# A diffusion trunk step on one core: prologue in three token spans, expert choice in two sorted halves between the output tiles, second norm applied to turned tiles

## The chip, the cores and the metric

The kernel runs on one core of one Trainium2 chip. The metric is device time in microseconds (us) of one execution; the time of a version is the median of several runs. TensorE (PE) does matrix products, VectorE (DVE) and ScalarE (ACT) element-wise work, GpSimd (POOL) here the indirect transfers and some adds, SyncE (SP) issues the other DMAs. The engines wait for each other through semaphores written out by hand.

## The reference

One layer over 128 context tokens and 1024 latent tokens of width 1024. What matters here is the start and the second half:

```python
mod = silu(cond) @ ada_w + ada_b
shift1, scale1, gate1, shift2, scale2, gate2 = split(mod, 6)
h = rmsnorm(x, norm1_g) * (1 + scale1) + shift1
proj = h @ w_in
...                                   # pooling branch, DeltaNet branch, merge -> mixed
x = x + gate1 * (mixed @ w_out)
h = rmsnorm(x, norm2_g) * (1 + scale2) + shift2
aff = softmax(h @ router_w)           # 16 experts
gates, idx = top_k(aff.T, cap)        # each expert picks cap = N/8 tokens of its set
ys = (silu(h[idx] @ w_gate) * (h[idx] @ w_up)) @ w_down * gates
x = x + gate2 * scatter_add(ys, idx)
```

Context and latent tokens have their own modulation (two condition vectors) and are separate routing sets: each of 16 experts picks 128 of 1024 latent tokens and 16 of 128 context tokens. A final RMSNorm follows. All is float32 but the inner solver of the DeltaNet.

## The kernel before

Tokens lie in nine tiles of 128 (tile 0 is context). The program is one long list per engine, and the order in each list is the order of execution.

**Prologue** (`prologue_pe`, `prologue_act`, `prologue_dve`, `sync1`). SP loads constants, then eight slabs of 1 MB of `ada_w` (set 0: shift1 and scale1), the nine tiles of x, the first head's weights, and sixteen more slabs (sets 1 and 2: gate1 and shift2, then scale2 and gate2), in a ring of four slots, so that slab n is issued when slab n-4 has been used. PE multiplies set 0; ACT computes the norms of all nine tiles (`act1`); PE turns the tiles so that channels lie on the partitions (`transpose_x`, three token spans of 128, 512 and 512, five banks); ACT and DVE apply scale and shift while they drain the banks (`modulate_act`, `modulate_dve`). Only when all are drained does PE start the first head's projections: units "q0" to "g1" of the tuple `FIRST` (letter: matrix, digit: span), with beta and alpha, decay sums and rows between them, and sets 1 and 2 at the end. `dve4_first` waits until sets 1 and 2 are written to `mod_dram`; ACT's drains of g0 and g1 wait for it.

**Heads, pooling, merge**: eight heads, and the mixed tensor. The change leaves their code alone.

**Step 7** (`pe7`, `act7`, `dve7`, `sync7`), for tile t = 0 to 8: PE projects tile t+1 (two halves of 512 columns); DVE multiplies by a broadcast row gate1 and adds x; ACT gets 1/rms; DVE multiplies by 1/rms and a row `amp2` and adds a row `shift2`; PE turns the result h2 (8 transposes); ACT drains it; PE multiplies it, as the stationary operand, by the router (16 columns). x goes to `x2_dram`, h2 to `h2_dram`.

**Step 8** (`dve8`, `act8`, `pe8`): softmax of all nine tiles at once, nine transposes, and then on DVE the choice over 16 partitions: 16 rounds over the 1024 latent tokens (maximum of 8, their indices, replace by -1), 2 rounds over the 128 context tokens.

**Step 9**, for each expert e: PE does 8 gate/up units, turns in the tokens of expert e+1 (`turn_in`), does 8 down units. ACT (`body9_act`) drains the turned tokens (`evac_in`) between its last Silu and the first drain of a down unit. The down units alternate between two banks: down unit 2 waits until ACT has drained down unit 0.

## Time and profile before

| | us |
|---|---|
| median of 3 runs | 2845.84 (2845.37 to 2846.87) |
| profiled execution, its own time | 2844.15 |
| its span in the trace | 2842.4 |
| PE busy in the span | 2577.6 (91%) |
| DVE busy | 1119.7 (39%) |
| ACT busy | 834.4 (29%) |

The span runs from the first to the last instruction of the trace. The busy shares are means over stages that have different limits; times below are counted from the start of the span. A matrix product in float32 shows as two records, so that a unit of eight products has "x16".

### The profile page before, as it was taken

The numbers are of one execution on the slowest core, as the hardware profiler recorded it, in microseconds if no ns is written. First come the engines' busy times: TensorE is split into PE (matmuls) and PEld (weight loads), VectorE is DVE, ScalarE is ACT, GpSimd is POOL, SyncE is SP. The second block draws the span as 40 slices with busy tenths as digits, with TensorE's granted clock in tenths as the row PEclk, the third lists the DMA queues.
The fourth block names the chain that finished last, engine by engine and source line by source line (L and its number), as shares of the span: only waits on it lengthen the run. The fifth ranks groups of instructions, "written<-read, shape, count | busy, mean of one in ns | idle before, by whom it ended". The sixth has DMA issues, their size and how long they took to land.

```text
span 2842.4 us, 42397 instructions
## 1 busy us (share of the span) xinstructions
PE 2577.6 (91%) x16072; PEld 1875.0 (66%) x16072; DVE 1119.7 (39%) x1996; ACT 834.4 (29%) x2081; POOL 303.2 (11%) x212
## 2 busy tenths in 40 slices
PE   5899999999989999899989999991799999999994
PEld 2355556565665656566555555440799999999994
DVE  2255565655656556565652353228110100101012
ACT  3133443444334353353442111110111112121112
POOL 0030030301203012030200000000010010101000
PEclk8999999999999999999999999995899999999997
DMA  8330200102002020110124233214478788787874
GB/s 294 149 94 19 73 17 18 58 19 73 17 24 64 6 73 17 55 36 3 59 85 153 96 114 104 96 74 185 174 247 296 263 279 303 248 299 247 293 268 150
DMA packets 197302, 365.30 MB, mean 129 GB/s; under 512 B 9006, under 2 KB 70387, under 8 KB 194083
## 3 DMA queue, kind: packets, MB, share of 16 engines
q1 hardware_dynamic: 190755, 344.41, 34.7%
q0 software_dynamic: 6400, 18.88, 2.7%
q8 instruction: 99, 1.62, 0.2%
q14 instruction: 48, 0.39, 0.0%
HBM read 322.59 MB, written 40.67 MB: 128 GB/s over the span
## 4 chain that ended last, share of the span: by engine, by line
PE 83%; DVE 6%; DMA 4%; issue 3%; ACT 2%; POOL 1%; SPq 1%; DVEq 0%; POOLq 0%; ACTq 0%
PE bank L563 25%; PE bank L1729 18%; PE bank L1743 9%; PE bank L733 6%; PE bank L1489 5%; PE bank L1277 4%; PE bank L1295 2%; PE bank L724 2%; DMA arena<-in_w_in 2%; PE bank L785 1%; PE bank L780 1%; PE bank L708 1%; PE bank L789 1%; PE bank L788 1%; DMA arena<-in_ada_w 1%
## 5 line engine op out<-in xcount | busy, mean ns | idle before, releaser
L563 PE MATMUL bank<-arena 128*128 128x512 f32 (+1 forms) x2496 | 874.1, 494 | 42.8 <-DVE arena L983 19.4
L563 PEld LDWEIGHTS bank<-arena 128*128 128x128 f32 x2496 | 394.1, 192 | 336.2 <-issue 298.7
L1729 PE MATMUL bank<-arena 128*128 128x144 f32 x4096 | 512.7, 286 | 1.5 <-ACT arena L1759 1.5
L1729 PEld LDWEIGHTS bank<-arena 128*128 128x128 f32 x4096 | 509.4, 190 | 1.7 <-ACT arena L1759 1.7
L1805 DVE TENSOR_TENSOR arena<-arena,bank 128x144 f32<-128x144 f32 x128 | 38.9, 304 | 702.7 <-ACT arena L1765 702.7
L873 ACT ACTIVATE arena<-bank 128x384 f16<-128x384 f16 (+1 forms) x504 | 205.9, 526 | 246.8 <-PE bank L724 246.6
L1743 PE MATMUL bank<-arena 128*128 128x144 f32 x2048 | 257.2, 286 | 0.7 <-DVE arena L1805 0.7
L1743 PEld LDWEIGHTS bank<-arena 128*128 128x128 f32 x2048 | 253.8, 189 | 1.9 <-DVE arena L1805 0.9
L733 PE MATMUL bank<-arena 128*128 128x128 f16 x2448 | 192.7, 220 | 6.5 <-ACT arena L873 0.2
L733 PEld LDWEIGHTS bank<-arena 128*128 128x128 f16 x2448 | 146.2, 98 | 67.9 <-ACT arena L873 36.8
L977 DVE CAST_PREDICATED arena<-arena,bank 128x384 f16<-128x384 uint32 x288 | 138.2, 553 | 99.5 <-PE bank L733 99.5
L1765 ACT ACTIVATE arena<-bank 128x144 f32<-128x144 f32 x128 | 37.2, 290 | 464.2 <-PE bank L1729 464.2
L594 ACT ACTIVATE arena<-bank 128x128 f32<-128x128 f32 (+1 forms) x156 | 77.1, 500 | 225.5 <-PE bank L563 185.4
L918 DVE SCALAR_TENSOR_TENSOR arena<-arena 128x1156 f32<-128x1156 f32 x96 | 136.3, 1420 | 5.9 <-issue 1.3
L1489 PE MATMUL bank<-arena 128*128 128x512 f32 x288 | 130.7, 614 | 1.7 <-DVE arena L1431 1.7
L969 DVE CAST arena<-bank 128x384 f16<-128x384 f32 x168 | 84.7, 552 | 118.4 <-PE bank L733 116.6
L1277 PE MATMUL bank<-arena 128*128 128x384 f32 x384 | 126.4, 491 | 0.7 <-DVE arena L1017 0.7
L1062 POOL TENSOR_TENSOR arena<-arena 128x1152 f32<-128x1152 f32 x8 | 29.5, 3689 | 826.2 <-ACT arena L895 826.2
L891 ACT ACTIVATE arena<-bank,arena 128x128 f32<-128x128 f32 x144 | 53.3, 370 | 190.9 <-PE bank L780 190.9
L1277 PEld LDWEIGHTS bank<-arena 128*128 128x128 f32 x384 | 73.4, 192 | 53.7 <-issue 3.2
L1489 PEld LDWEIGHTS bank<-arena 128*128 128x128 f32 x288 | 55.6, 195 | 70.9 <-issue 70.9
L1771 ACT ACTIVATE arena<-bank,arena 128x128 f32<-128x128 f32 x128 | 47.0, 367 | 177.3 <-PE bank L1743 177.3
(243 smaller groups left out, 2657.4 us busy)
## 6 DMA issues: line engine op xcount, KB each, us to landing
arena<-in_exp_w_gate SPq DMA_DIRECT2D x32, 2048.0 KB, 10.5
arena<-in_exp_w_up SPq DMA_DIRECT2D x32, 2048.0 KB, 15.6
arena<-in_exp_w_down SPq DMA_DIRECT2D x32, 2048.0 KB, 10.8
arena<-in_w_in SPq DMA_DIRECT2D x52, 512.0 KB, 6.8
arena<-in_ada_w SPq DMA_DIRECT2D x24, 1024.0 KB, 8.1
side_dram<-arena SPq DMA_DIRECT2D x20, 576.0 KB, 3.2
arena<-side_dram SPq DMA_DIRECT2D x20, 576.0 KB, 3.9
arena<-g_dram SPq DMA_DIRECT2D x16, 576.0 KB, 5.2
```

What stands on the lines that cost most here:

```text
L563: ins = nc.tensor.matmul(unit_bank(order, name)[:, 0:n], w[:, k, :], hT3[:, k, at:at + n], start=(k == 0), stop=(k == KD - 1))
L594: nc.scalar.activation(dst, bank[:, 0:n], ACT.Copy).then_inc(sem("pj_drained"), 1)
L724: last = nc.tensor.transpose(TRI[d][g].bitcast(F16)[:, i * P:(i + 1) * P], src[d][:, 3 * g + i, :], ident_h)
L733: last = nc.tensor.matmul(TRI[d][g][:, i * P:(i + 1) * P], lhs if lhs.shape[1] == P else lhs[:, 3 * g + i, :], rhs if rhs.shape[1] == P el ...
L873: nc.scalar.activation(flat(dst[d], g), src[:, 0:384], ACT.Copy).then_inc(sem(f"drained{d}_act"), 1)
L918: ins = nc.vector.scalar_tensor_tensor(qkvg[j][:, 0:CW], raw[j][:, tap:tap + CW], w, qkvg[j][:, 0:CW], ALU.mult, ALU.add)
L969: nc.vector.tensor_copy(flat(Zs[1], g), TRI[1][g][:, 0:384]).then_inc(sem("drained1_dve"), 1)
L977: nc.vector.copy_predicated(Ys[d][:, 3 * g:3 * g + 3, :], masks[:, 1 - d, lv + 1, :].unsqueeze(1).to_broadcast([P, 3, P]), TRI[d][g][:, 0: ...
L1277: last = nc.tensor.matmul(banks[n % RING][:, 0:CH], w_dn[half][:, k, col:col + P], bT3[:, k, c * CH:(c + 1) * CH], start=(k == 0), stop=(k ...
L1489: last = nc.tensor.matmul(banks[2 * (t % 2) + half][:, 0:512], mixT3[:, k, t * P:(t + 1) * P], w_outs[:, k, half * 512:(half + 1) * 512], ...
L1729: last = nc.tensor.matmul(banks[3 + f % 2][:, m * CAP:(m + 1) * CAP], w_unit[2 * half + m][:, k, col:col + P], xsT[:, k, :], start=(k == 0 ...
L1743: last = nc.tensor.matmul(banks[5 + dt % 2][:, 0:CAP], w_unit[4 + half][:, k, col:col + P], hid[:, k, :], start=(k == 0), stop=(k == KD - 1))
```

## The change

In the prologue each token span is normed, turned, drained and projected by itself, x tiles and head weights are loaded in that order, the slabs of sets 1 and 2 are multiplied in pieces between the projections, and only gate1 goes through `mod_dram`: shift2 and amp2 = (1 + scale2) * norm2_g are kept with channels on the partitions. In step 7 tiles run in the order 1 to 8, 0 (`TILE`); ACT writes x/rms, that is turned, and amp2 and shift2 are applied by ACT as scale and bias of eight ACTIVATEs per tile; the router is stationary in four groups of 32 columns, and `sel4` adds the four groups. The choice runs in three groups (tiles 1 to 4, 5 to 8, context), its rounds are written between the residuals of later tiles, and the two sorted lists of 128 are merged by one comparison of the first with the second read backwards. Since `xn_dram` holds x/rms alone, `evac_in` applies amp2 and shift2 to every expert's tokens too.

```diff
-        HB = 5
+        HB = 4
+        SPAN_USES = (range(0, KD), range(KD, 2 * KD), range(2 * KD, 3 * KD))
...
-        FIRST = ("q0", "q1", "q2", "v0", "v1", "v2", "k0", "k1", "k2", "g0", "g1")
+        FIRST = ("q0", "q1", "v0", "v1", "k0", "k1", "q2", "v2", "k2", "g0", "g1")
...
-            dve.wait_ge(sem("mod_saved"), 16 * NCG * (N_SETS - 1))
+            dve.wait_ge(sem("mod_saved"), 16 * (NCG // 2))
...
+        def turn_x(i):
+            pe.wait_ge(sem("xn_ready2"), i + 1)
...
+        def route(i):
+            pe.wait_ge(sem("h2T_ready"), i + 1)
             for k in range(KD):
-                last = nc.tensor.matmul(banks[6][:, t * E:(t + 1) * E], h2T[t % XR][:, k, :], router[:, k, :], start=(k == 0), stop=(k == KD - 1))
+                j = k % NCG
+                last = nc.tensor.matmul(banks[7][CG * j:CG * (j + 1), 0:P], router[:, k, :], h2T[i % XR][:, k, :], start=(k < NCG), stop=(k >= KD - NCG))
...
+        def logits(i):
+            pe.wait_ge(sem("routed_ready"), i + 1)
+            nc.tensor.matmul(LOGITS[:, i * E:(i + 1) * E], routed[i % 2], sel4[:, 0:E], start=True, stop=True).then_inc(sem("logits_filled"), 1)
...
+            nc.scalar.activation(xn_t[s], x_t[s], ACT.Copy, scale=rstd[i % 2]).then_inc(sem("xn_ready2"), 1)
+            if i == NL2:
+                routes_exp(act, 0)
+            act.wait_ge(sem("h2T_filled"), i + 1)
+            for k in range(KD):
+                last = nc.scalar.activation(h2T[s][:, k, :], banks[4 + k // 4][:, (k % 4) * P:(k % 4 + 1) * P], ACT.Identity,
+                                            scale=amp2T[:, c, k:k + 1], bias=modT3[:, c, 3 * KD + k:3 * KD + k + 1])
...
-            nc.vector.scalar_tensor_tensor(h2_t[s], x_t[s], rstd[t % 2], row["amp2"][c], ALU.mult, ALU.mult).then_inc(sem("h2_scaled"), 1)
-            nc.vector.tensor_tensor(h2_t[s], h2_t[s], row["shift2"][c], ALU.add).then_inc(sem("h2_ready"), 1)
...
+        for i in range(NL2 + 1):
+            residual(i)
+        shift_logits(0)
+        affinities(0)
+        take_affinities(0)
+        rounds(0, 0, 4)
+        residual(NL2 + 1)
+        rounds(0, 4, 10)
+        residual(NL2 + 2)
+        rounds(0, 10, ROUNDS)
+        residual(NL2 + 3)
+        step(nc.vector.tensor_copy(idxf3[0][0:E, :], idxu3[0][0:E, :]))
+        shift_logits(1)
+        affinities(1)
+        take_affinities(1)
+        rounds(1, 0, 2)
+        residual(2 * NL2)
+        rounds(1, 2, 8)
+        shift_logits(2)
+        affinities(2)
+        rounds(1, 8, ROUNDS)
+        take_affinities(2)
+        rounds(2, 0, CAP_C // 8)
...
     def evac_in(act, e):
         act.wait_ge(sem("xsT_filled"), e + 1)
-        for b in range(2):
-            nc.scalar.activation(xsT[:, 4 * b:4 * b + 4, 0:CAP_L], banks[b][:, 0:512].rearrange("p (k c) -> p k c", k=4), ACT.Copy)
-        for j in range(NJ):
-            last = nc.scalar.activation(xsT_c[:, :, j, :], banks[2][:, j * QROWS:(j + 1) * QROWS].rearrange("p (q c) -> p q c", q=NQ), ACT.Copy)
+        for k in range(KD):
+            nc.scalar.activation(xsT[:, k, 0:CAP_L], banks[k // 4][:, (k % 4) * P:(k % 4 + 1) * P], ACT.Identity,
+                                 scale=amp2T[:, 1, k:k + 1], bias=modT3[:, 1, 3 * KD + k:3 * KD + k + 1])
+        for k in range(KD):
+            q, j = k // NJ, k % NJ
+            last = nc.scalar.activation(xsT[:, k, CAP_L:CAP], banks[2][:, j * QROWS + q * CAP_C:j * QROWS + (q + 1) * CAP_C], ACT.Identity,
+                                        scale=amp2T[:, 0, k:k + 1], bias=modT3[:, 0, 3 * KD + k:3 * KD + k + 1])
         last.then_inc(sem("xsT_ready"), 1)
```

How the order moves, at three places. First PE in the prologue, from the end of set 0 on, before (L264 turns x, L563 is a projection, L330 beta and alpha):

```order
L264 MATMUL bank<-arena 128x128 x72
L563 MATMUL bank<-arena 128x128 x8
L563 MATMUL bank<-arena 128x512 x16
L330 MATMUL bank<-arena 32x128 x8
L330 MATMUL bank<-arena 32x512 x16
```

The same place in the change (L270 turns x, L584 is a projection, L244 a piece of a set, L336 beta and alpha):

```order
L270 MATMUL bank<-arena 128x128 x8
L584 MATMUL bank<-arena 128x128 x8
L270 MATMUL bank<-arena 128x128 x32
L584 MATMUL bank<-arena 128x512 x8
L584 MATMUL bank<-arena 128x128 x8
L584 MATMUL bank<-arena 128x512 x8
L244 MATMUL bank<-arena 32x512 x12
L584 MATMUL bank<-arena 128x128 x8
L584 MATMUL bank<-arena 128x512 x8
L270 MATMUL bank<-arena 128x128 x32
L336 MATMUL bank<-arena 32x128 x8
L336 MATMUL bank<-arena 32x512 x16
```

Five units of projection and three slabs now stand ahead of the last span's transposes. Second, PE in step 7, one tile before (L1489 output projection, L1501 transposes, L1505 router):

```order
L1489 MATMUL bank<-arena 128x512 x16
L1501 MATMUL bank<-arena 128x128 x8
L1505 MATMUL bank<-arena 128x16 x8
L1489 MATMUL bank<-arena 128x512 x16
L1501 MATMUL bank<-arena 128x128 x8
```

One tile in the change (L1566 half a projection, L1575 transposes, L1583 router in groups, L1589 their sum):

```order
L1566 MATMUL bank<-arena 128x512 x8
L1589 MATMUL bank<-arena 128x16
L1575 MATMUL bank<-arena 128x128 x8
L1566 MATMUL bank<-arena 128x512 x8
L1583 MATMUL bank<-arena 32x128 x8
```

Half a projection now lies between the transposes and the router that needs them drained. Third, ACT in step 9 between the last Silu of an expert and its first down units, before (L1757 and L1759 are `evac_in`, L1771 and L1772 the drain of a down unit):

```order
L1765 ACTIVATE arena<-bank 128x144
L1755 REGISTER_ALU
L1757 ACTIVATE arena<-bank 128x4x128 x2
L1759 ACTIVATE arena<-bank 128x4x16 x2
L1771 ACTIVATE arena<-bank,arena 128x128
L1772 ACTIVATE arena<-bank,arena 128x16
```

and in the change (L1915 and L1919 are `evac_in`, L1932 and L1933 the drain of a down unit):

```order
L1926 ACTIVATE arena<-bank 128x144
L1913 REGISTER_ALU
L1915 ACTIVATE arena<-bank,arena 128x128 x8
L1919 ACTIVATE arena<-bank,arena 128x16 x8
L1932 ACTIVATE arena<-bank,arena 128x128
L1933 ACTIVATE arena<-bank,arena 128x16
```

Sixteen instructions with scale and bias from memory stand where four plain copies stood.

## Rows read from the trace of the kernel before

**Rows 1.** Busy time by stretch (us): PE, PEld, DVE, ACT, POOL, PEclk, DMA share

```profile
1755.00:1927.00 172.00, 157.82 (x504) 82.46 (x504) 47.98 (x49) 24.61 (x54) 0.00 (x0) 0.94 0.21 77
2057.00:2107.00 50.00, 50.00 (x407) 49.76 (x406) 4.66 (x16) 9.18 (x29) 5.11 (x5) 1.00 0.81 279
```

**Rows 2.** Timeline, PE in the prologue: start, us, engine, line, count, idle before

```profile
44.80 8.96 PE L264 MATMUL bank<-arena 128*128 128x128 f32 x67 [12.34 <-DVE arena L282]
...
70.37 4.08 PE L330 MATMUL bank<-arena 128*32 128x128 f32 x48
...
109.31 3.64 PE L241 MATMUL bank<-arena 128*32 128x512 f32 x32
115.38 1.33 PE L241 MATMUL bank<-arena 128*32 128x512 f32 x8 [2.44 <-DMA arena<-in_ada_w]
...
153.33 8.94 PE L563 MATMUL bank<-arena 128*128 128x512 f32 x16 [1.49 <-ACT arena L594]
162.11 2.11 PE L690 MATMUL bank<-arena 128*128 128x128 f32 x6
```

**Rows 3.** Timeline, ACT and DVE in the prologue

```profile
41.95 1.04 ACT L362 ACTIVATE arena<-arena 128x1024 f32<-128x1024 f32 x1
...
43.55 0.44 ACT L273 ACTIVATE arena<-bank,arena 128x128 f32<-128x128 f32 x1
...
43.89 0.45 ACT L273 ACTIVATE arena<-bank,arena 128x128 f32<-128x128 f32 x1
...
152.82 0.06 DVE L1029 MEMSET arena<- 128x1 f32 x1 [0.70 <-DMA mod_dram<-arena]
```

**Rows 4.** Chain that ended last: start, us, one projection unit of 512 columns

```profile
94.66 6.87 PE bank L563 x16
```

**Rows 5.** Timeline, PE in step 7, one tile

```profile
1800.72 1.03 PE L1501 MATMUL bank<-arena 128*128 128x128 f32 x8
1802.93 1.96 PE L1505 MATMUL bank<-arena 128*128 128x16 f32 x16 [1.18 <-ACT arena L1519]
1804.74 15.68 PE L1489 MATMUL bank<-arena 128*128 128x512 f32 x32
```

**Rows 6.** Timeline, DVE and ACT in step 7, the same tile

```profile
1800.92 1.29 DVE L1535 TENSOR_TENSOR arena<-bank,arena 128x512 f32<-128x512 f32 x2 [10.96 <-PE bank L1489]
...
1801.79 1.09 ACT L1519 ACTIVATE arena<-bank 128x512 f32<-128x512 f32 x2 [14.41 <-PE bank L1501]
1803.50 1.06 ACT L1512 ACTIVATE arena<-arena 128x1024 f32<-128x1024 f32 x1 [0.63 <-DVE arena L1539]
...
1805.25 1.29 DVE L1544 SCALAR_TENSOR_TENSOR arena<-arena 128x1024 f32<-128x1024 f32 x1 [1.78 <-ACT arena L1516]
```

**Rows 7.** Timeline, step 8: rounds over 1024 and 128 tokens, PE after them

```profile
1932.38 1.22 DVE L1591 MAX8 arena<-arena 16x8 f32<-16x1024 f32 x1
...
1936.26 1.22 DVE L1591 MAX8 arena<-arena 16x8 f32<-16x1024 f32 x1
...
1993.18 0.28 DVE L1591 MAX8 arena<-arena 16x8 f32<-16x128 f32 x1
...
1994.26 0.28 DVE L1591 MAX8 arena<-arena 16x8 f32<-16x128 f32 x1
...
1996.11 0.28 PE L1617 MATMUL bank<-arena 16*128 16x16 f32 x1 [65.28 <-DVE arena L1600]
```

**Rows 8.** Timeline, PE and ACT of expert 0, from the down units on

```profile
2041.62 16.08 PE L1743 MATMUL bank<-arena 128*128 128x144 f32 x128
...
2041.73 1.09 ACT L1757 ACTIVATE arena<-bank 128x512 f32<-128x512 f32 x2 [0.85 <-PE bank L1705]
2042.70 0.35 ACT L1759 ACTIVATE arena<-bank 128x64 f32<-128x64 f32 x2
2043.90 0.37 ACT L1771 ACTIVATE arena<-bank,arena 128x128 f32<-128x128 f32 x1 [0.85 <-PE bank L1743]
2044.17 0.27 ACT L1772 ACTIVATE arena<-bank,arena 128x16 f32<-128x16 f32 x1
```

More of the change, by code:

```diff
@@ L1446, in later @@
     at_word[0] = BACK_AT
-    h2_t = [take(D) for _ in range(XR)]
+    xn_t = [take(D) for _ in range(XR)]
     prod = [take(D) for _ in range(XR)]
     h2T = [take(D).rearrange("p (k t) -> p k t", k=KD) for _ in range(XR)]
+    routed = [take(P) for _ in range(2)]
     assert at_word[0] <= BACK_AT + 2 * NG * T
@@ L1482, in pe7 @@
         pe.wait_ge(sem("mix_drained"), MIX_ALL)
-        def project(t):
-            if t >= 2:
-                pe.wait_ge(sem("y_drained"), t - 1)
-            for half in range(2):
-                for k in range(KD):
-                    last = nc.tensor.matmul(banks[2 * (t % 2) + half][:, 0:512], mixT3[:, k, t * P:(t + 1) * P], w_outs[:, k, half * 512:(half + 1) * 512], start=(k == 0), stop=(k == KD - 1))
-            last.then_inc(sem("y_filled"), 1)
-        project(0)
-        pe.wait_ge(sem("rows_in"), 16 * 8)
@@ L1494, in pe7, with project @@
-        for t in range(NT):
-            if t + 1 < NT:
-                project(t + 1)
-            pe.wait_ge(sem("h2_ready"), t + 1)
-            if t > 0:
-                pe.wait_ge(sem("h2T_ready"), t)
+        def project(i, half, ks=range(KD)):
+            t = TILE[i]
+            if i >= 2 and half == 0 and ks[0] == 0:
+                pe.wait_ge(sem("y_drained"), i - 1)
+            for k in ks:
+                last = nc.tensor.matmul(banks[2 * (i % 2) + half][:, 0:512], mixT3[:, k, t * P:(t + 1) * P], w_outs[:, k, half * 512:(half + 1) * 512], start=(k == 0), stop=(k == KD - 1))
+            if half == 1 and ks[-1] == KD - 1:
+                last.then_inc(sem("y_filled"), 1)
@@ new lines, in turn_affinities @@
+        def turn_affinities(g):
+            pe.wait_ge(sem("aff_ready"), g + 1)
+            for n, i in enumerate(GROUPS[g]):
+                last = nc.tensor.transpose(AFF_BANK[g][0:E, n * P:(n + 1) * P], af3[:, i, :], ident)
+            last.then_inc(sem("affT_filled"), 1)
+        FIRST_K, LAST_K = range(0, KD // 2), range(KD // 2, KD)
+        ENDS = (NL2 - 1, 2 * NL2 - 1, NT - 1)
+        project(0, 0)
+        project(0, 1)
+        pe.wait_ge(sem("rows_in"), ROWS_ALL)
+        for i in range(NT):
+            if i + 1 < NT:
+                if i == NL2:
+                    project(i + 1, 0, FIRST_K)
+                    turn_affinities(0)
+                    project(i + 1, 0, LAST_K)
+                else:
+                    project(i + 1, 0)
+            if i > 0 and i - 1 not in ENDS:
+                logits(i - 1)
+            turn_x(i)
+            if i + 1 < NT and i != ENDS[1]:
+                project(i + 1, 1)
+            route(i)
+            if i in ENDS:
+                logits(i)
+            if i == ENDS[1]:
+                project(i + 1, 1, FIRST_K)
+                turn_affinities(1)
+                project(i + 1, 1, LAST_K)
@@ new lines, in residual @@
+        def residual(i):
+            c, s = min(TILE[i], 1), i % XR
+            dve.wait_ge(sem("y_filled"), i + 1)
+            if i >= 2:
+                dve.wait_ge(sem("rstd2"), i - 1)
+            for half in range(2):
+                last = nc.vector.tensor_tensor(prod[s][:, half * 512:(half + 1) * 512], banks[2 * (i % 2) + half][:, 0:512], gate1_row[c][:, half * 512:(half + 1) * 512], ALU.mult)
+            last.then_inc(sem("y_drained"), 1)
+            dve.wait_ge(sem("y_drained"), i + 1)
+            dve.wait_ge(sem(f"xt_in{s}"), 16 * (i // XR + 1))
+            nc.vector.tensor_tensor(x_t[s], x_t[s], prod[s], ALU.add).then_inc(sem("x1_ready"), 1)
@@ new lines, in dve7, with rounds @@
+        ROUNDS = CAP_L // 8
+        def rounds(g, r, to):
+            for r_ in range(r, to):
+                top_round(g, r_)
+        for i in range(NL2 + 1):
[10 more added lines that the diff above has]
+        step(nc.vector.tensor_copy(idxf3[0][0:E, :], idxu3[0][0:E, :]))
@@ L1601, in dve8 @@
+        last.then_inc(*reach("topk_ready"))
+    at_word[0] = ROUTE_END
+    def dve8(dve):
         dve.wait_ge(*at_step("topkT_filled"))
```

403 lines of the change are left out of this document (227 added, 176 removed).

## Prediction, made before the change was run

> **What bounds the kernel now.** I read the busy time by stretch first, then the timelines of the three places that the change touches, and last the chain of work that ended last, for unit prices. In the experts PE is busy for all 50.00 of 50.00 us with the granted clock at 1.00, so any new wait there is paid in full; in step 7 it is busy for 157.82 of 172 [rows 1], and the 14 us left are waits that an order can remove. In the choice DVE alone works: PE sits idle for 65.28 us and resumes at 1996.11 [rows 7]. In the prologue PE waits 12.34 us for the norms, later 2.44 us and less for slabs of `ada_w`, and the unit before the first head's attention work starts at 153.33 [rows 2]. So three stages can give time, and one, the experts, can only take it.
>
> **The prologue.** Prices: a unit of 512 columns 6.87 us [rows 4], one of 128 columns a quarter plus a little, 2.05; a slab 3.64/4 = 0.91; all transposes with their drains 9 to 10 us from 44.80, so 4.3 for a span of 512; beta and alpha 4.08 [rows 2]. ACT norms a tile in 1.6 us (41.95 to 43.55) [rows 3], and the first begins where it did. Counting back from 43.55, tile 0 is normed at 30.8; its span is drained by 34.3, q0 runs to 36.4, tiles 1 to 4 are normed at 41 and their span is drained by 45.6. From there PE has q1, v0, v1 (15.8), three slabs (2.7), k0, k1 (8.9), the last span (4.3), beta and alpha (4.1), three slabs (2.7), q2 (6.9), the token columns (an estimate, 2.1), two slabs (1.8), v2 (6.9), sums and turned shift2 (1.7, estimate), three slabs (2.7), k2 (6.9) and decay rows (1.1, estimate): 68.6, to 114.2. DVE's convolutions of q and v lie beside these. Slab 23 can be issued when slab 19 is used, at 115.2; slab 12 was used 5 us after slab 8 had freed its slot (110.2 to 115.38) [rows 2], so it is used by 121.2; DVE's part and PE's turn of it take 3, g0 and g1 8.9, g2 6.9: 140. Before, that point was 162.11 [rows 2]. The wait of `dve4_first` for `mod_dram` [rows 3] is now for two small writes issued earlier, and what it holds back (ACT's drains of g0, g1) is wanted only at 133. The gain is 22; since PE idles more in short pieces at the start, and its first records after idle time can be slow, I take **-21**. Bounds: -14 if the slabs land late or the clock stays at the lower level through the second span, -25 if nothing waits for slabs.
>
> **Step 7.** Before, a tile costs 13.74 of projection, 1.03 of transposes, 1.18 of waiting for ACT and 1.96 of router, 17.9 in all; in some tiles the projection takes 15.68, because its first records run at half speed behind that wait [rows 5]. In the change the drain (eight instructions) lies beside half a projection. The router is now 8 products of 128 columns in four groups: beta and alpha had 9216 product-columns of that kind in 4.08 [rows 2], so 1024 cost 0.5; the sum over groups 0.25. A tile costs 15.6. DVE's residual takes 1.29 and about 1.25, ACT's 1/rms 1.75 (1803.50 to 1805.25) [rows 6] and its product about 1.1, 5.5 from the end of the projection to x/rms, against 7.4 that PE has to do before it wants it: no wait. With the start at 1755.3 the fifth tile's projection ends at 1755.3 + 13.9 + 14.8 + 3 x 15.6 = 1830.8. Call this Y.
>
> **The choice.** A round over 1024 tokens takes 1936.26 - 1932.38 = 3.88, one over 128 takes 1.08 [rows 7]. The line between them gives 2.28 for 512, so 32 rounds take 71.5 where 16 took 61; but the first half is beside the projections. Step by step from Y: residual to +2.7; shift, Exp (ACT does it after its product, +5.9), normalising to +6.9, transposes and copy to +8.2 (PE waits 2.1 here); 4 rounds to +17.3; tile 5's projection ends at +18.9, residual to +21.5; 6 rounds to +35.2, residual to +37.9; 6 rounds to +50.9, residual to +53.6. The second list then needs tile 7: PE turns it at +58.8, waits 3 for ACT's eight drains, and has its logits at +63.1; affinities, four products, transposes and copy to +67.7. Now DVE is the end: 2 rounds to +72.3, residual of tile 8 to +74.9, 6 rounds to +88.6, context's affinities to +90.5, 8 rounds to +108.0, context's copy and rounds to +110.3, the merge (16 small copies, some seven short steps, the quarter tables) 4, an estimate: +114.3, or 1945.1. Before, PE resumed at 1996.11 [rows 7]: **-51**. Bounds: the merge between 2 and 8; if the small steps wait longer each, -45; -54 at best. Expert 0's weights are issued 40 us earlier too, with tile 8's stores, and still land before they are used; their tail can meet the first gather: **+1**, between 0 and +3.
>
> **The experts, where the price is.** `evac_in` was 4 plain drains: the first of 512 columns at 2041.73, the 64-column ones from 2042.70, all over by 2043.05, long before down unit 0 was full at 2043.7 [rows 8]. Now it is 8 of 128 columns and 8 of 16, each with scale and bias from memory. Rows of the first kind stand in the prologue: 0.44 long, and the next begins 0.34 later [rows 3]. Of the second there is none. A 128-column drain with a scale alone is 0.37 and its 16-column neighbour 0.27, the neighbour starting 0.27 after it, so they overlap by 0.10 [rows 8]; the bias adds 0.07, and I take 0.34 long and 0.24 apart. Together 8 x 0.34 + 8 x 0.24 = 4.64: ACT is free at 2046.37 and has drained unit 0 at 2046.37 + 0.27 + 0.27 = 2046.91. PE resumes 0.05 behind such a release (ACT's end at 1802.88, PE at 1802.93) [rows 5, 6], so at 2046.96. It wanted the bank two units of 16.08/8 = 2.01 after 2041.62 [rows 8], at 2045.6. The wait is 1.4; unit 1's drain is in time again. Fifteen experts pay it, **+21**, and the one ahead of expert 0 pays 4.64 - 1.3 = **+3.3**. Bounds: if the bias cost nothing (0.27 and 0.17 apart) 0.25 each, +4; if these instructions did not overlap at all (0.44 and 0.34) 3.0 each, +45. I take the middle because it is built on the one row of the very form.
>
> The Trainium skill (ScalarE: Activation LUTs, What ACT_TABLE_LOAD costs) says that an ACTIVATE with immediate operands takes 186 ns + 0.833 ns per element, each pointer operand adds about 93 ns, and neighbours overlap by about 93. By that, an estimate, the sixteen take 5.4 us, the wait is 2.2 and the fifteen cost 32 rather than 21; the one row that there is, 0.44 where the rule has 0.48 [rows 3], lies below it, and I stay with the row.
>
> **Sum.** -21 - 51 + 1 + 21 + 3 = -47 on the execution's own 2844.15, which is 1.7 below the median: 2797, or **2799** as a median of runs. Heads, pooling, merge and the last norm keep their code and their times.
>
> **The rivals.**
> - *The rounds don't hide* (DVE in the way of the tiles): a residual behind a block of rounds comes late, PE waits for `y_drained` or for x/rms, and the whole choice stands behind the tiles. For it: 6 rounds are 13.7 us in a tile of 15.6 with 2.6 of residual, no slack. Against: PE needs x/rms only after the next half projection. If all is in a row the tiles take 139 and affinities, rounds and merge 85, 224 in place of 241: 2833.
> - *Each wait in the experts also drops PE's clock.* In step 7 a wait of 1.18 and 1.96 of 16-column products are followed in some tiles by slow records that cost 1.8 [rows 5]. If that comes with every expert it is 15 x 1.8 = 27 more: 2826. Against: there the wait stands beside products of few columns, here between full ones.
> - *A wait of 2.2 in the experts*: if a 16-column drain with both operands costs as much as a 128-column one, the sixteen take 16 x 0.34 = 5.4 us, and fifteen waits 33: 2811. For it: nearly all of so short a drain is fixed cost; against: 0.37 and 0.27 do differ [rows 8]. (The Trainium skill's rule above comes to about the same time.)
> - *No wait in the experts*, because ACT packs sixteen short drains closer than any row shows: 24 less, 2777.
> - *Slower.* The same mechanism on the other side: the experts must lose more than 47 us beyond what I have given them, 71 in 15 waits, that is 4.5 each, which needs `evac_in` at 7.8 us, 0.49 an instruction. The longest row of such a form is 0.45 [rows 3]. From that point on the change is slower, say 2855.
> - *The prologue gives nothing*, since the slabs, not PE, set its end: 2820. Against: with all slabs asked for late, PE waited for one no longer than 2.44 [rows 2].
>
> **How the numbers follow.** The forecast, all gains and a wait of about 1.4 an expert, 0.48, its own range 2788 to 2810; a wait of 2.2 or more 0.20; rounds that don't hide 0.08; clock drops 0.08; no wait 0.07; prologue flat 0.05; slower 0.04. The range 2780 to 2826 leaves out the no-wait case, most of the unhidden rounds and the slower case, 0.2. Measurement can tell 0.2%, 6 us, from no change: faster 0.94, the same 0.02, slower 0.04.
>
> **What would show it.** Right: g2 of the first head's prologue starting near 133; a PE tile of about 15.6 with no wait between transposes and router; a 512-token round of 2.28; PE resuming near 190 us after step 7's start; in every expert one PE wait near 1.4 released by ACT before the third down unit, an expert 1.4 longer than before. Wrong: a DVE wait of PE inside a tile other than the fifth and the eighth, granted clock under 1.00 in the experts, or sixteen drains that take other than 4.6.

## The result, and the profile after

| | before | after |
|---|---|---|
| median of runs | 2845.61 (4 runs, 2844.7 to 2846.87) | 2812.24 (4 runs, 2806.7 to 2816.53) |
| ratio, 95% interval | | 0.9876 [0.9863, 0.9889] |
| profiled execution, its own time | 2844.15 | 2813.57 |
| its span | 2842.4 | 2811.7 |

The change makes the kernel 33 us faster. The forecast was 2799, so the direction and the wide range (2780 to 2826) held, but the narrow one (2788 to 2810) did not, and the gain came out 13 us smaller. By the time alone this could as well be the rival with a wait of 2.2 us in the experts, which asked for 2811; the stages decide between them. Four single executions took 3114 to 6860 us where others of the same kernel took 2807 to 2853, and no median or ratio here counts them.

The sum over the stages of the two profiled executions (after minus before, in span time):

| stretch | forecast | measured |
|---|---|---|
| start to the first square of head 0 | -21 | -18.2 (177.42 to 159.24) |
| from there to the end of head 7 | 0 | +8.0 (1375.8 to 1383.8) |
| step 7 and choice | -51 | -49.5 (240.77 to 191.27) |
| gather, and the drains ahead of expert 0 | +4.3 | +5.0 |
| fifteen experts | +21 | +23.6 |
| all | -47 | -31 |

Busy time by stretch of the changed kernel, step 7 and one expert (columns as in [rows 1]):

```profile
1745.21:1917.21 172.00, 146.71 (x531) 69.75 (x531) 82.84 (x174) 54.40 (x129) 0.00 (x0) 0.92 0.26 94
2038.76:2090.19 51.43, 50.13 (x405) 49.68 (x406) 4.64 (x16) 12.58 (x41) 5.08 (x5) 1.00 0.78 268
```

In the first 172 us of step 7 DVE was busy for 47.98 [rows 1] and is now for 82.84: the rounds have moved in beside the projections. The expert lasts 51.43 and PE is busy for 50.13 of it, at clock 1.00.

Timeline of PE in the prologue (L584 is a projection, L270 a turn, L244 a slab, L711, the head's attention work, what was L690 [rows 2]), then of ACT (L374 is the norm of a tile, L280 the drain of turned tiles):

```profile
36.21 3.75 PE L584 MATMUL bank<-arena 128*128 128x128 f32 x16 [0.60 <-DVE arena L289]
43.44 6.00 PE L270 MATMUL bank<-arena 128*128 128x128 f32 x32 [3.48 <-DVE arena L438]
50.40 15.76 PE L584 MATMUL bank<-arena 128*128 128x512 f32 x48 [0.96 <-ACT arena L280]
...
124.99 1.07 PE L244 MATMUL bank<-arena 128*32 128x512 f32 x8 [2.84 <-DMA arena<-in_ada_w]
...
144.65 2.10 PE L711 MATMUL bank<-arena 128*128 128x128 f32 x6
```

```profile
34.18 0.82 ACT L280 ACTIVATE arena<-bank,arena 128x128 f32<-128x128 f32 x2 [3.03 <-PE bank L270]
...
36.01 1.05 ACT L374 ACTIVATE arena<-arena 128x1024 f32<-128x1024 f32 x1
```

PE projects q0 8.6 us before the point at which it used to turn x (44.80 [rows 2]), but q0's 16 records take 3.75 where 16 of the same form take 1.95 from 146.59 on, and the second span's turns start 2.4 later than reckoned. ACT began the norms of the second span only at 36.01, when it had drained the first.

Timeline of PE and DVE in step 7 and the choice (L1566 projection, L1575 turn of x/rms, L1583 router, L1589 sum of its groups, L1595 turn of affinities, L1709 a round's MAX8, L1777 the first product after the choice; step 7 starts at 1745.21):

```profile
1812.52 1.07 PE L1575 MATMUL bank<-arena 128*128 128x128 f32 x8
1813.43 7.03 PE L1566 MATMUL bank<-arena 128*128 128x512 f32 x16
1820.39 0.65 PE L1583 MATMUL bank<-arena 128*32 128x128 f32 x16
...
1826.91 0.60 PE L1595 MATMUL bank<-arena 128*16 128x128 f32 x4 [1.55 <-DVE arena L1697]
...
1881.48 1.08 PE L1583 MATMUL bank<-arena 128*32 128x128 f32 x16 [2.99 <-ACT arena L1648]
...
1883.41 5.94 PE L1566 MATMUL bank<-arena 128*128 128x512 f32 x8
...
1936.48 0.28 PE L1777 MATMUL bank<-arena 16*128 16x16 f32 x1 [23.55 <-DVE arena L1762]
```

```profile
1828.26 0.68 DVE L1709 MAX8 arena<-arena 16x8 f32<-16x512 f32 x1
...
1830.55 0.68 DVE L1709 MAX8 arena<-arena 16x8 f32<-16x512 f32 x1
...
1883.68 0.23 DVE L1689 TENSOR_REDUCE arena<-bank 128x4 f32<-128x64 f32 x1 [10.68 <-PE bank L1589]
...
1889.82 0.68 DVE L1702 COPY arena<-bank 16x512 f32<-16x512 f32 x1 [4.64 <-PE bank L1595]
```

A tile takes 15.55 (start of one tile's transposes to the next, 1796.97 to 1812.52), a round over 512 tokens 2.29, and PE resumes 191.27 after the start of step 7, with nearly the steps and waits that the forecast listed (1.55 for its 2.1, 2.99 for its 3). DVE idles 10.68 and 4.64 us before the second half's rounds: there the tiles are the bound, not the rounds.

Timeline of ACT and PE from the end of expert 1's gate and up units on (expert 0's down units start at 1987.22 and have the same rows; L1915 and L1919 are `evac_in`, L1932 and L1933 the drain of a down unit, L1900 a down unit):

```profile
2038.76 2.90 ACT L1915 ACTIVATE arena<-bank,arena 128x128 f32<-128x128 f32 x8 [0.85 <-PE bank L1862]
2041.51 2.19 ACT L1919 ACTIVATE arena<-bank,arena 128x16 f32<-128x16 f32 x8
2043.50 0.46 ACT L1932 ACTIVATE arena<-bank,arena 128x128 f32<-128x128 f32 x1
...
```

```profile
2038.65 4.22 PE L1900 MATMUL bank<-arena 128*128 128x144 f32 x32
2044.18 6.07 PE L1900 MATMUL bank<-arena 128*128 128x144 f32 x47 [1.30 <-ACT arena L1933]
```

The sixteen drains take 2043.50 - 2038.76 = 4.74 (forecast 4.64), and PE waits 1.30 before its third down unit (forecast 1.4), where before it went on without a gap [rows 8]. Its third down unit starts 5.53 after its first (2044.18 - 2038.65), where two units take 4.02 [rows 8], so it is 1.51 late. From down unit 0 of expert 0 to that of expert 15 it is 771.06 us, before 747.49: 1.57 an expert, of which 1.30 is the wait and 0.27 lies around it.

### The profile page after: what moved, and what is told of

Its sections match the earlier page's. It is cut to its first block, busy times and chain, and to the rows that moved or that the text cites. A ratio compares the mean times of both kernels' runs of the same rounds, so it can differ in the third digit from the quotient of the medians.

```text
span 2811.7 us, 42808 instructions
## 1 busy us (share of the span) xinstructions
PE 2571.4 (91%) x16094; PEld 1869.9 (67%) x16094; DVE 1108.8 (39%) x2093; ACT 918.8 (33%) x2347; POOL 303.2 (11%) x212
## 4 chain that ended last, share of the span: by engine, by line
PE 81%; DVE 6%; ACT 5%; issue 3%; DMA 3%; SPq 1%; POOL 1%; DVEq 0%; POOLq 0%; ACTq 0%
PE bank L584 25%; PE bank L1886 18%; PE bank L1900 7%; PE bank L754 6%; PE bank L1321 4%; PE bank L1566 4%; PE bank L1339 2%; PE bank L745 2%; ACT arena L1915 2%; PE bank L806 1%; DMA arena<-in_w_in 1%; PE bank L801 1%; PE bank L729 1%; ACT arena L1919 1%; PE bank L810 1%
## 5 line engine op out<-in xcount | busy, mean ns | idle before, releaser
L584 PE MATMUL bank<-arena 128*128 128x512 f32 (+1 forms) x2496 | 876.5, 495 | 44.1 <-DVE arena L1004 19.5
L584 PEld LDWEIGHTS bank<-arena 128*128 128x128 f32 x2496 | 396.7, 193 | 337.2 <-issue 301.5
L1900 PE MATMUL bank<-arena 128*128 128x144 f32 x2048 | 261.3, 287 | 20.2 <-ACT arena L1933 19.5
L1900 PEld LDWEIGHTS bank<-arena 128*128 128x128 f32 x2048 | 254.6, 189 | 24.7 <-ACT arena L1933 22.7
L1566 PE MATMUL bank<-arena 128*128 128x512 f32 x288 | 129.7, 603 | 1.7 <-DVE arena L1476 1.7
L1932 ACT ACTIVATE arena<-bank,arena 128x128 f32<-128x128 f32 x128 | 49.2, 390 | 149.8 <-PE bank L1900 149.8
L1566 PEld LDWEIGHTS bank<-arena 128*128 128x128 f32 x288 | 54.0, 192 | 65.4 <-issue 65.4
```

Source lines behind the costliest of these rows:

```text
L584: ins = nc.tensor.matmul(unit_bank(order, name)[:, 0:n], w[:, k, :], hT3[:, k, at:at + n], start=(k == 0), stop=(k == KD - 1))
L1566: last = nc.tensor.matmul(banks[2 * (i % 2) + half][:, 0:512], mixT3[:, k, t * P:(t + 1) * P], w_outs[:, k, half * 512:(half + 1) * 512], ...
L1900: last = nc.tensor.matmul(banks[5 + dt % 2][:, 0:CAP], w_unit[4 + half][:, k, col:col + P], hid[:, k, :], start=(k == 0), stop=(k == KD - 1))
```

## The experiments

Every kernel is the changed kernel with the edit shown, unless said otherwise. Ratios are to the kernel before, run beside it; the changed kernel's is 0.9876.

**The price in the experts.** First the four old copies:

```diff
-        for k in range(KD):
-            nc.scalar.activation(xsT[:, k, 0:CAP_L], banks[k // 4][:, (k % 4) * P:(k % 4 + 1) * P], ACT.Identity,
-                                 scale=amp2T[:, 1, k:k + 1], bias=modT3[:, 1, 3 * KD + k:3 * KD + k + 1])
...
+        for b in range(2):
+            nc.scalar.activation(xsT[:, 4 * b:4 * b + 4, 0:CAP_L], banks[b][:, 0:512].rearrange("p (k c) -> p k c", k=4), ACT.Copy)
...
```

> The changed kernel with the four plain drains of the kernel before in `evac_in`; scale and shift of the experts' inputs are left out. If the operand-bearing drains are the whole price of the experts (a wait of 1.57 us in 15 of them and 5.0 instead of 1.3 us ahead of expert 0), this is 15 x 1.57 + 3.7 = 27 us faster than the changed kernel, about 2785, with an expert every 49.86 us and no wait of PE for L1919 or the down units' drains. If the longer expert period came from something else that the change moved (weights that land later, the gather from the new tensor), the period stays at 51.4 and the time at 2808 or more.

Measured: 2782.14 us, ratio 0.9776 [0.9761, 0.9791]; no PE wait in the experts' down units, 49.85 an expert. Between the medians the new drains cost 30 us; by the stages' rows 27 (23.6 in the experts and 3.6 ahead of expert 0). Then the number of instructions kept and only their operands changed (`ACT.Identity` with scale and bias to `ACT.Copy`, all sixteen):

> Sixteen drains of the same sizes as in the change, but with no operand from memory; scale and shift are left out. If the operands make the drains long (an estimate from the rows of plain drains: 0.18 apart for 128 columns, 0.09 for 16), all sixteen take 2.2 us and the experts show no wait, 49.9 each. If the number of instructions makes them long, they take over 3.3 us and a wait of 0.2 us or more stays.

Measured in one execution: 2778.47 us, an expert 49.85, no wait in the down units. Timeline of ACT in expert 1 (L1915 and L1918 are the drains, L1930 the next down unit's):

```profile
2025.41 1.47 ACT L1915 ACTIVATE arena<-bank 128x128 f32<-128x128 f32 x8 [0.85 <-PE bank L1862]
2026.68 0.81 ACT L1918 ACTIVATE arena<-bank 128x16 f32<-128x16 f32 x8
2027.59 0.37 ACT L1930 ACTIVATE arena<-bank,arena 128x128 f32<-128x128 f32 x1
```

Sixteen drains without pointer operands (operands read from memory, one value for each partition) take 2.18 us, with them 4.74: the two operands are 0.16 us an instruction, as far as this run can tell, since the function changed with them from Identity to Copy. The split into sixteen alone would have cost PE nothing in the fifteen experts and 0.8 us ahead of expert 0 (a wait of 2.23 there, 1.47 with the four copies). Next the eight 16-column drains given to DVE, as `tensor_scalar` with the same two operands, and a second semaphore that PE waits for:

```diff
+    def drain_in(dve, e):
+        dve.wait_ge(sem("xsT_filled"), e + 1)
...
+        for k in range(KD):
+            q, j = k // NJ, k % NJ
+            last = nc.vector.tensor_scalar(xsT[:, k, CAP_L:CAP], banks[2][:, j * QROWS + q * CAP_C:j * QROWS + (q + 1) * CAP_C],
+                                           amp2T[:, 0, k:k + 1], modT3[:, 0, 3 * KD + k:3 * KD + k + 1], ALU.mult, ALU.add)
+        last.then_inc(sem("xsT_ready_dve"), 1)
```

> ACT drains the eight latent blocks, DVE the eight 16-column context blocks behind its last product of the expert, with the same scale and shift. If ACT is late only by the length of its own list, 8 x 0.34 = 2.75 us end before the down unit's drain is wanted, the wait is gone: 23.6 us faster than the changed kernel in the experts and 2 ahead of them, 2786 to 2790. If the wait had another cause, the time stays near 2812.

Measured: 2782.73 us (2782.06 to 2785.54), ratio 0.9777 [0.9762, 0.9792]: 63 us faster than before and some 29 faster than the changed kernel, with the whole computation in it. The stages' rows give 25.6 of it (23.6 in the experts, and ahead of expert 0 a wait of 3.05 for 5.09); the rest, and that the time lies 3 us below the range expected, is no more than one execution differs from the next (below). Timelines of DVE, ACT and PE in expert 1:

```profile
2031.64 1.71 DVE L1963 TENSOR_SCALAR arena<-bank,arena 128x16 f32<-128x16 f32 x8 [0.51 <-PE bank L1862]
...
2031.64 2.90 ACT L1916 ACTIVATE arena<-bank,arena 128x128 f32<-128x128 f32 x8 [0.85 <-PE bank L1862]
2034.39 0.40 ACT L1929 ACTIVATE arena<-bank,arena 128x128 f32<-128x128 f32 x1
...
2031.53 16.07 PE L1901 MATMUL bank<-arena 128*128 128x144 f32 x128
```

The eight down units are one unbroken piece again. With four of the 128-column drains on DVE too, so that ACT keeps four of them and DVE does twelve instructions:

> ACT drains four latent blocks, DVE the other four and the context. The wait is gone in the same way as with only the context moved, so the experts take the same 49.9 each; ahead of expert 0 ACT takes 1.4 and DVE about 8 x 0.17 + 4 x 0.3 = 2.6 us rather than 5.0, so 1 us or less is left between this and the version with only the context moved: 2786 to 2789. If DVE's added work (2.6 us behind its last product) came in the way of what it does for the gather or the weighing, the experts would be longer than 49.9.

Measured: 2783.03 us (2778.64 to 2790.13), ratio 0.9775 [0.9761, 0.9788], an expert 49.85: once PE doesn't wait, an earlier end of the drains is worth nothing. Ahead of expert 0 PE waits 3.24, no less than the 3.05 with the context alone on DVE.

**Whether the rounds are hidden.** The first half's rounds, and two of the second's, behind the last residual:

```diff
-        rounds(0, 0, 4)
-        residual(NL2 + 1)
...
+        for i in range(NL2 + 1, 2 * NL2):
+            residual(i)
...
         residual(2 * NL2)
+        rounds(0, 0, ROUNDS)
...
+        rounds(1, 0, 8)
```

> The changed kernel with the sixteen rounds of the first half, and the two of the second half that stood before the last residual, moved behind the last residual; all the rest of the order, the merge too, stays. Theory: those rounds are hidden beside PE's projections, 18 x 2.28 = 41 us of DVE, of which at most 2 to 4 us filled a time in which DVE would have worked anyway; PE resumes after the choice about 228 to 232 us after step 7's start instead of 191.3, and the kernel takes 2812 + 39 = 2851 us, a little more than before the change (2845.6), since sixteen rounds of 3.88 us are now thirty-two of 2.28. Rival 1: the rounds between the residuals hold the tiles up as much as they hide, then the time stays within 5 us of 2812. Rival 2: half of it, because the affinities of the second half wait for the same DVE: 2830.

Measured: 2844.12 us, ratio 0.9985 [0.9975, 0.9995]. Timeline of PE, start of step 7 and end of the choice:

```profile
1739.82 20.84 PE L1566 MATMUL bank<-arena 128*128 128x512 f32 x48 [1.68 <-DVE arena L1476]
...
1970.04 0.29 PE L1773 MATMUL bank<-arena 16*128 16x16 f32 x1 [23.55 <-DVE arena L1758]
...
1977.13 1.97 PE L1856 MATMUL bank<-arena 128*128 128x128 f32 x8 [6.59 <-DMA arena<-xn_dram,arena]
```

PE resumes 230.22 after step 7's start, 39 later, as expected; both rivals fall. So without the overlap two lists are worth nothing: thirty-two rounds over 512 (2.29 each) are longer than sixteen over 1024 (3.88 [rows 7]). Of the 49.5 us that step 7 and choice gained, 39 are this overlap; the other 10.5 stay when it is gone. The time missed the 2851 expected by 7: it rose by 32 and not 39. Between the two profiled executions that is 5.7 us of shorter heads (below) and a gather that waits 6.59 where the changed kernel's waits 8.00. The rows say what the gather meets. Busy time from the end of the choice to the first tokens, the changed kernel and then this one (the last two figures are the DMA engines' busy share and GB/s):

```profile
1937.00:1945.00 8.00, 0.01 (x1) 0.02 (x1) 0.61 (x6) 0.00 (x0) 2.09 (x2) 0.50 0.85 315
```

```profile
1970.50:1977.00 6.50, 0.04 (x1) 0.00 (x0) 0.61 (x6) 0.00 (x0) 2.09 (x2) 0.50 0.30 91
```

The kernel before has 0.31 and 91 at its gather too, and waits 6.58: in both the experts' weights have landed, in the changed kernel they are still landing.

**The router's form.**

```diff
-                last = nc.tensor.matmul(banks[7][CG * j:CG * (j + 1), 0:P], router[:, k, :], h2T[i % XR][:, k, :], start=(k < NCG), stop=(k >= KD - NCG))
+                last = nc.tensor.matmul(LOGITS[:, i * E:(i + 1) * E], h2T[i % XR][:, k, :], router[:, k, 0:E], start=(k == 0), stop=(k == KD - 1))
...
-            nc.scalar.activation(routed[i % 2], banks[7][:, 0:P], ACT.Copy).then_inc(sem("routed_ready"), 1)
```

> The changed kernel with the router's products in the old form: the turned tile as the stationary operand and 16 columns of router weights, eight to a tile, with no sum over column groups and no copy between. Theory: PE pays 1.96 us where it pays 0.65 + 0.29 = 0.94, so 1.0 more in a tile, about 7 up to the last tile on which the second list of candidates depends, and where the short products are followed by a stretch at half clock some 2 more each: 2819 to 2825. Rival 1: PE's time in a tile is not what the end of the choice hangs on (DVE is), then only the tiles up to the fifth and the eighth count through their waits, and the time moves by less than 3: 2812 to 2815. Rival 2: the copy and the second product that fall away give back as much as the 16-column form costs, and the kernel becomes faster: under 2808.

Measured: 2815.29 us, ratio 0.9886 [0.9867, 0.9904], not to be told from the changed kernel's 0.9876, and 4 us below the range expected. Timeline of PE:

```profile
1769.33 1.85 PE L1582 MATMUL bank<-arena 128*128 128x16 f32 x16
...
1936.52 0.29 PE L1770 MATMUL bank<-arena 16*128 16x16 f32 x1 [23.55 <-DVE arena L1755]
```

A tile takes 16.39 rather than 15.55, and PE resumes 195.6 after step 7's start (1740.91), 4.3 later. By the time alone this is the edge of the first rival (under 3 us); by the trace the theory's price per tile is there (0.84 for 1.0) and reaches the end of the choice, but the half-clock stretches that it counted on did not come inside the tiles, where no wait stands ahead of the router.

**What the prologue's gain is made of.** All three spans together before the first projection, and, apart from it, spans kept but the slabs of sets 1 and 2 in two blocks at the end:

```diff
 spans together
             transpose_x(pe, 0)
-            h_drained(pe, KD)
-            unit()
             transpose_x(pe, 1)
...
+            transpose_x(pe, 2)
+            h_drained(pe, 3 * KD)
...
 slabs last
-            ada_set(pe, 1, range(0, 3))
...
+            ada_set(pe, 1, range(KD))
...
+            ada_set(pe, 2, range(KD))
```

> The changed kernel with the three spans of the prologue done one step at a time for all (norms of all tiles, then all turns, then scale and shift of all), and only then the projections; the slabs of ada_w stay between the projections as in the change. Theory: the spans themselves give PE little, because the start that they allow is spent at half clock (q0's 16 products of 128 columns in 3.75 and the second span's 32 turns in 6.00 us). PE turns all tiles from about 44.8 to 54.7, then projects; the four units that ended at 66.1 end at 72.4, and the last span's turns, 4.6 with their wait, are no longer ahead: +1.7 at the end, the first turn of the head's attention work (144.65) moves to about 146.5, and the kernel takes 2814, 2812 to 2818. Rival: the spans are what gave the 17.5 us, then that point moves to 156 or later and the kernel takes 2823 or more.

> The changed kernel with the sixteen slabs of ada_w's second and third set taken in two blocks of eight near the end of the prologue, as before the change, and the spans kept. Theory: what the prologue gained came mostly from the slabs standing between the projections. PE waits for slabs again as it did before the change: 2.44, 1.14, 0.57 and 0.55 in the first block, 2.60, 1.43, 0.81 and 0.53 in the second, 0.82 and 1.49 after them, 12.4 in all, where the changed kernel has 2.84 + 1.27 = 4.1; the head's attention work, first at 144.65, begins at about 153, and the kernel takes 2820, 2817 to 2825. Rival: the spans are what gave the time and the slabs' place none, then it takes 2812 within 3.

Measured: 2811.8 us (three executions, 2811.3 to 2818.9), ratio 0.9888 [0.9859, 0.9916], and 2822.38 us, ratio 0.9905 [0.988, 0.9929]. By the time alone spans would be worth nothing, but the profiled execution of that kernel had heads 9.7 us shorter than the changed kernel's (below), so this is read from the prologue's rows. The busy time from the start to the first L711 (before: L690), in order of the kernels before, changed, spans together, slabs last:

```profile
0.00:162.11 162.11, 118.42 (x547) 52.95 (x548) 46.87 (x88) 38.23 (x80) 0.20 (x4) 0.87 0.61 223
```

```profile
0.00:144.65 144.65, 116.02 (x551) 57.27 (x552) 47.42 (x92) 39.20 (x80) 0.20 (x4) 0.89 0.74 260
```

```profile
0.00:151.55 151.55, 114.47 (x552) 54.82 (x553) 47.22 (x92) 39.40 (x80) 0.20 (x4) 0.88 0.70 248
```

```profile
0.00:157.71 157.71, 122.16 (x551) 55.13 (x552) 47.55 (x92) 39.10 (x80) 0.20 (x4) 0.88 0.65 236
```

Length less PE's busy time is its idle time: 43.7, 28.6, 37.1 and 35.6. Of the 17.5 us that the change takes off, 15.1 are idle time. Spans together cost 6.9 us at this point, not the 1.7 expected and not the 11 or more of the rival. PE went on turning at 48.95 and not at 44.80 [rows 2], because ACT stood twice for tiles of x, 1.29 us ahead of tile 1 and 2.22 ahead of tile 5. ACT's and PE's rows of that kernel:

```profile
41.27 1.06 ACT L374 ACTIVATE arena<-arena 128x1024 f32<-128x1024 f32 x1 [2.22 <-DMA arena<-in_x_sample]
...
48.95 9.40 PE L270 MATMUL bank<-arena 128*128 128x128 f32 x68 [14.35 <-DVE arena L289]
```

This kernel keeps the change's order of loads, so 6.9 is the worth of the spans under that order; what they would be worth with x loaded as before was not run.

Slabs in blocks cost 13.1: 7 of idle time, close to what the waits of the two blocks say (2.50, 1.44, 0.56, 0.55 and 2.39, 1.44, 0.56, 0.57, with 1.9 behind them, in place of 2.84 and 1.27), and 6 of products at the lower clock, which the trace has from 112.8 to 119.6 and from 136.6 to 153.7, where PE stood between slabs.

The four lengths can be read from the other end too. From the kernel before (162.11), the slabs' place gives 10.6 (to 151.55) and the spans, with the order of loads, 4.4 (to 157.71). So the slabs' place is worth the more whichever is counted first, 10.6 to 13.1 us, and the spans 4.4 to 6.9.

**Where 8 us went in the heads.** Kernels before and changed once more, and both with four idle repeats of one turn (`turn_part(pe, banks[0], part[2])`, in the changed kernel into `banks[5]`), meant to let the heads begin later:

> The kernel before with PE's turn of the last part of the modulation repeated four more times, so that the heads begin about 2 us later and nothing in them is changed. Question: where did 8 us of the changed kernel's gain go between the first head's start and the end of the last, code that the change does not touch? Theory: into short stretches of half clock, 3.4 us each in the records. From the ten profiles so far the eight heads last 1370.6 + 1.77 x (number of such records between 200 and 1500 us), within 3 us: before 1375.8 with 4, the changed kernel 1383.8 with 7, others between 1374.1 with 2 and 1384.4 with 8, and which number an execution gets is not set by the change. Then the heads here last as that line says for the number found, between 1372 and 1386, not necessarily 1375.8. Rival: the change itself makes each head slower (its weights come later, a queue is fuller); then a kernel before keeps 1376 within 1 whatever its start, and the time is 2848 within 1.

> The changed kernel with the same four turns added, the heads 2 us later. Theory: the heads' length follows the number of half-clock records by the line of the ten profiles, 1370.6 + 1.77 each, between 1372 and 1386, and moves by up to 8 us from one execution or small shift to the next. Rival, the change itself slows each head: 1383.8 again within 1.

> The kernel before, profiled once more. Theory of the half-clock records: its heads, 1375.8 us with 4 such records in the first profile, lie on the same line, 1370.6 + 1.77 each, and their number can be another. Rival, a fixed length that belongs to the kernel: 1375.8 within 0.5.

> The changed kernel, profiled once more. Theory: its heads are on the line 1370.6 + 1.77 for each half-clock record, and as 2806.7 to 2816.5 us was the spread of its first four runs, this profile can have between 2 and 8 of them. Rival: 1383.8 within 0.5 again, the kernel's own length.

Measured: 2844.6 us, ratio 1.0001 [0.9989, 1.0013]; 2806.9 us, ratio 0.986 [0.984, 0.9879]; 2848.46 and 2812.98 in one execution each. The changed kernel's heads did begin 1.7 us later (160.91), the kernel before's did not (176.85, for 177.42 and 178.56 without the repeats), so that one counts as another execution and no more. The heads' code is the same in all fourteen profiles. Their length from head 0's first square to PE's last wait behind head 7, and the number of stretches of 3.4 us in them in which the granted clock was 0.50:

| profile | stretches | heads, us |
|---|---|---|
| before; again; later | 4; 4; 4 | 1375.8; 1378.5; 1376.2 |
| changed; again; later | 7; 6; 4 | 1383.8; 1380.6; 1375.6 |
| spans together; slabs last | 2; 4 | 1374.1; 1380.5 |
| rounds last; router in rows | 4; 6 | 1378.1; 1380.5 |
| four copies; sixteen copies | 6; 3 | 1380.4; 1374.8 |
| context on DVE; half on DVE | 5; 8 | 1380.0; 1384.4 |

The best line through them has 1.8 us for each stretch, about the half of 3.4 that half a clock would cost; thirteen lie within 1.8 us of it and one (slabs last) 3.1 above. The last four profiles (before later, changed later, before again, changed again) came out at -1.5, -2.1, +0.8 and -0.6 from the line stated before them. The rival, a length of the kernel's own, falls with 1375.6 and 1380.6 for the changed kernel and 1378.5 for the kernel before; before later, 1376.2, fits both.

PE's busy time over the heads says it more sharply than the length. It is 1281.8 us with 2 stretches, 1283.4 with 3, 1284.8 to 1285.2 in all six profiles with 4, 1286.8 with 5, 1288.1 to 1288.4 with 6, 1290.0 with 7 and 1291.5 with 8: 1.63 us a stretch, and no profile is more than 0.3 from that line. The rest of the scatter is idle time, 90.5 to 95.3 us. Busy and idle time of the two profiles compared, before and after:

```profile
177.42:1553.20 1375.78, 1284.76 (x7874) 817.84 (x7873) 780.38 (x1354) 573.18 (x1401) 221.93 (x128) 0.99 0.14 44
```

```profile
159.24:1543.00 1383.76, 1290.05 (x7875) 821.08 (x7874) 780.14 (x1354) 573.41 (x1401) 221.92 (x128) 0.99 0.14 44
```

So of the 8.0 us 5.3 are products at half clock and 2.7 are idle, of which 2.5 are PE's six waits for the heads' weights (8.1 us before, 10.6 after). Those waits are 8.0 to 10.3 in the three profiles of the kernel before and 7.5 to 10.6 in the eleven with the new prologue, so they too are no mark of the change.

What such a stretch looks like, first the changed kernel's clock and PE at the start of its fifth head, then PE at the same place before:

```profile
850.00:854.00 4.00, 4.00 (x15) 2.83 (x14) 0.00 (x0) 3.45 (x6) 0.00 (x0) 0.57 0.71 174
```

```profile
849.04 2.63 PE L584 MATMUL bank<-arena 128*128 128x128 f32 x16 [2.15 <-DMA arena<-in_w_in]
851.46 3.23 PE L711 MATMUL bank<-arena 128*128 128x128 f32 x6
```

```profile
862.10 2.05 PE L563 MATMUL bank<-arena 128*128 128x128 f32 x16 [1.76 <-DMA arena<-in_w_in]
863.99 2.11 PE L690 MATMUL bank<-arena 128*128 128x128 f32 x6
```

PE had stood for the next head's weights in both; the same six records take 3.23 nearly all at half clock and 2.11 at full. In the changed kernel each of the seven stretches begins within 1.5 us of the end of a PE wait of 1.9 to 2.8: two for weights, five for DVE in the middle of a head. But that wait for DVE, 2.39 or more, stands once in every head of both kernels, and has a stretch behind it in five of eight heads here and in three of eight before. What decides between them no run shows.

## Why the prediction was right, and where its sizes were off

- *The prologue.* -18.2 for -21. Already the first span was drained 1.7 late (36.0, reckoned 34.3), because its eight turns ran at half clock and started behind DVE's work on scale and shift. That alone would have cost nothing, but ACT's norms of the second span stand behind this drain, so its turns began at 43.44 (reckoned 41), and they too ran at half clock (6.00 for the 3.66 of the last span's), so the projections began at 50.40 and not 45.6. These 4.8 us stand nearly unchanged at the last slab (used by 126.1, reckoned 121.2) and at the head's attention work (144.65, reckoned 140): what lies between was sized right within 1 us. For the same reason g2 started at 137.8 and not near 133. The text saw the risk and took 1 us for it; the trace has PE at half clock from 20.9 to 48.2. What hangs on the slabs and what on the spans is shown by the two experiments.
- *The heads.* This is the step that failed: "Heads, pooling, merge and the last norm keep their code and their times". They keep their code; this execution's heads took 8.0 longer, 5.3 of it in products, three stretches at half clock more, and 2.5 in longer waits for weights. Which execution gets how many is not the change's doing alone: the changed kernel ranges over 8 us (with its later start counted in), and its four timed runs over 10. Whether the change makes them likelier is open: the three profiles with the old prologue average 1376.8 with 4 stretches each, the eleven with a new one 1379.3 with 2 to 8, and the spread is as large. Half of the shortfall of 16 us in the table is this, and one profile could not have told it from a price of the change. In an execution with four stretches the forecast would have been within 8 us (changed later: 2806.9), in this one it was 13 off: part of the distance is chance.
- *Step 7 and choice.* -49.5 for -51, with the fifth tile's projection done 75.3 after the start (75.5 forecast). The 1.5 us too little lie between tile 7's logits (63.1 after the fifth tile's projection, as forecast) and the second half's first round (70.0 for 67.7), because half a projection there ran at half clock behind the wait for ACT (5.94 for 3.6); 0.8 us was made good elsewhere. The merge took 4.5 (4 forecast). That it is the hiding and not the split that pays is shown: 39 us are lost again when the rounds stand behind the tiles.
- *Gather and weights.* +1.4 for +1, and for the reason given: the gather meets the weights' tail (DMA share 0.85, and 0.30 where the gather comes 37 us later after step 7's start and waits 6.59).
- *Experts.* +23.6 for +21, ahead of expert 0 +3.6 for +3.3. The price of sixteen drains came from one row of the very form, 0.34 apart [rows 3] (measured 2.75/8 = 0.344), and from 0.24 for a form without a row (0.249). PE's third down unit was 1.51 late for 1.4, as ACT ended 0.1 later, and each expert lost 1.57. The granted clock is 1.00 from 1956.5 to 2778, so the rival of clock drops falls, and with 1.30 in the trace the one of 2.2 us too. The Trainium skill (ScalarE: Activation LUTs, What ACT_TABLE_LOAD costs) puts about 93 ns on each pointer operand and gives, an estimate, 5.4 us for the sixteen. The trace has 4.74; two operands cost 0.19 at 128 columns, as by that rule, and 0.14 at 16, less than by it. So the row was the better guide for the sum, and the rule had the right kind of cost.
- *Slower* needed 0.49 an instruction; 0.34 is the most that stands there. (The text's 71 us in 15 waits are 4.7 each and not 4.5, which changes nothing.)

## What to carry over

When an elementwise step is moved from rows to turned tiles, look for every other reader of the rows: here a gain of 50 us in step 7 and the choice came with a bill of 27 in a stage where PE was 100% busy, and 25.6 of it vanished when eight of the sixteen drains went to an engine that idled there. Price short drains by their spacing with the operands that they will have, and compare it with the time until the engine behind them wants its bank. A forecast of one part in a hundred should carry a range for stages that the change doesn't touch: here some 10 us between executions, mostly stretches at half clock. To tell such scatter from a price of the change, compare PE's busy time over the untouched stage with the number of half-clock stretches in it.

## What the runs showed of the hardware

- ACT from a bank, spacing of neighbours: 128 columns 0.16 us plain and 0.344 with scale and bias from memory, 16 columns 0.11 and 0.25. Scale and bias from memory (with Identity for Copy) cost 0.14 to 0.19 us, more than the 112 columns between the two forms (0.05 plain, 0.10 with the operands).
- DVE's 16-column TENSOR_SCALAR with two such operands stands 0.20 apart (1.63 for eight, in the kernel with the context on DVE).
- Half-clock stretches of 3.4 us fall between heads and inside them, 2 to 8 in 1380 us, in executions of the same code; each adds 1.63 us to PE's busy time (fourteen profiles, none more than 0.3 off). In the changed kernel all seven begin at a PE wait of 1.9 to 2.8 us, and other waits of 2.39 in the same code have none behind them.
- While the experts' weights were landing (DMA share 0.85) the first gather kept PE waiting for 8.00 us; with the DMA engines at 0.30 it was 6.59.
